# GpSimd makes 18 of the 198 low parts of the expert weights, VectorE the others

## Chip, core, metric

The kernel runs on one core of a Trainium2 chip. The metric is the device time of one execution in microseconds, the median of some runs. All arithmetic is float32 at the interface. TensorE multiplies in a reduced 32-bit format (fp32r), so the kernel splits each float32 operand into a high part, which is a copy in that format, and a low part, the rest, and adds two or three products.

## What is computed

Two residual layers. Each has a token mixer (gated short convolution beside latent attention). The first is followed by a dense SwiGLU, the second by eight SwiGLU experts of which each token uses two. The part that matters here is the last:

```
def moe_swiglu(x, w_router, w_gate, w_up, w_down):
    logits = (t @ w_router)
    top_vals, top_idx = lax.top_k(logits, 2)
    top_w = jax.nn.softmax(top_vals, axis=-1)
    gates = sum(one_hot(top_idx, 8) * top_w[..., None], axis=1)
    for e in range(8):
        out = out + gates[:, e:e+1] * ((silu(t @ w_gate[e]) * (t @ w_up[e])) @ w_down[e])
```

256 tokens, width 1024, expert width 1792. All eight experts' weights, 176 MB, are read once from memory.

## The kernel before

Each engine has its own program; nothing but semaphores orders them. Layer 0 and the mixer of layer 1 take the first 690 us or so. The expert part follows and is what the change touches.

**Steps and granules.** Experts are sorted on the chip by how many tokens chose them. The three with most tokens are computed for 128 tokens (large), the other five for 64 (small). Each expert is worked in two halves of its width of 1792; a half is a step k, 16 steps in a round. Steps 0, 1, 6, 7, 12, 13 are of large experts, 2 to 5, 8 to 11, 14 and 15 of small ones. One round serves all tokens unless an expert has too many; rounds 1 and 2 exist as code and are not run here. A granule is what one DMA loads: 128 rows of the gate matrix (n = 0 to 7) or of the up matrix (n = 8 to 15) with the 896 columns of this half, 448 KB, or 128 rows of the down matrix with 1024 columns (n = 16 to 22, 512 KB). Step k's list of granules is its 16 gate and up granules and then the seven down granules of step k - 1. The list of the round, GRANULES, has 368 entries.

**The path of a granule.** SP loads it into one of 12 raw slots (`expert_loads`). ACT copies it to the high part, in one of 8 weight slots (`expert_hi`, L943). DVE subtracts the high part from the raw one and writes the low part (`expert_lo`, L1491). PE multiplies with both. ACT and DVE take two neighbours at once where both have the same width: this is a split (SPLITS, 198 in the round), 128x1792 for gate and up, 128x2048 for down; where the widths differ each goes alone. The high part of a split waits for its loads and for PE's use of the granules that held the weight slots eight granules before. The low part waits for the high part (`e_hi_made`). PE waits for the low part (`e_lo_made`, counted in the order of the splits). SP's next load into a raw slot waits for the low part of the granule that lay there twelve before, and SP issues loads in their order, so that the loads behind a waiting one wait as well.

**DVE's order** is written out by its loop over the granules: at every second granule i it makes the low part of the split that is eight ahead, and between these stand the operations that drain the banks: `expert_hidden` (hid_buf, L1630, silu(gate) times up), `hidden_lo_half` (hT, L1636 and L1640, the low part of the transposed hidden values), `output_lo` (y_lo, L1613), `add_output` (h, L1620) and `choose` (sel, L1596). Each of these but the last has one input in PSUM; a low part L1491 reads raw and w_hi, both in SBUF. **GpSimd (POOL)** does small things for the norms, and in the expert part nothing until the final norm (L721).

## Time and profile before

| | |
|---|---|
| median of 3 runs | 1156.25 us (1156.22 to 1157.06) |
| the profiled execution | 1157.23 us, span 1155.4 us, granted clock 0.998 |
| busy over the span | PE 1125.5 us (97%), DVE 878.4 (76%), ACT 753.7 (65%), POOL 35.0 (3%) |
| costliest group of the expert part | L1491 on DVE, w_lo and w_lo_more, 198 operations, 383 us |
| chain that ended last | PE 75%, DVE 18%, DMA 3%, ACT 2% |

In the profile's rows a time is in microseconds from the start of the span, a duration in microseconds or, where marked ns, nanoseconds. "x2" is how many instructions a row holds. The records of DVE operations that follow each other overlap by some 0.07 us, so what one costs its engine is the distance from start to start. A busy PE is not PE at its peak, since the ends of its matmuls are modelled.

### The profile page before, as it was taken

To read this page: it belongs to the slowest core of one execution; us is meant where nothing else is said; L and a number is where in the kernel's file an instruction comes from. 1 tells how busy PE (TensorE), PEld (TensorE's weight loads), DVE (VectorE), ACT (ScalarE), POOL (GpSimd) and SP (SyncE) were. 2 spreads that over 40 slices of the span, in tenths; PEclk is the share of its full clock that TensorE was granted. 3 is DMA by queue.
4 is the path that set the end of the run, shared out by engine and by line. 5 is a ranking of instruction groups with operands and counts; after the bars stand their busy time and mean duration, and the time that the engine had idled before them with its cause. 6 is when DMAs were issued, how large, how long until landed. Compare 5 with 4: busy or idle time off the path is not lost.

```text
span 1155.4 us, 15714 instructions
## 1 busy us (share of the span) xinstructions
PE 1125.5 (97%) x5556; PEld 944.9 (82%) x5556; DVE 878.4 (76%) x986; ACT 753.7 (65%) x936; POOL 35.0 (3%) x64
## 2 busy tenths in 40 slices
PE   8999999999999999999999999999899999999997
PEld 7888788888888888888788888887778887888885
DVE  6568667665454555468667669999999899999997
ACT  6555566545444345555566556799987798988785
POOL 3001000000000001001001000000000000000000
PEclk9999999999999999999999999999999999999999
DMA  8845433668556344645433556999999999999993
GB/s 302 298 135 182 146 103 111 190 210 305 186 183 198 114 169 145 213 135 182 147 101 133 189 202 221 390 386 407 407 407 395 369 399 401 406 407 405 406 370 155
DMA packets 120555, 294.96 MB, mean 255 GB/s; under 512 B 9007, under 2 KB 33677, under 8 KB 119965
## 3 DMA queue, kind: packets, MB, share of 16 engines
q1 hardware_dynamic: 119376, 288.66, 69.3%
q0 software_dynamic: 960, 5.28, 1.2%
q8 instruction: 42, 0.69, 0.2%
q14 instruction: 37, 0.30, 0.1%
q10 hardware_dynamic: 140, 0.04, 0.0%
HBM read 292.90 MB, written 1.05 MB: 254 GB/s over the span
## 4 chain that ended last, share of the span: by engine, by line
PE 75%; DVE 18%; DMA 3%; ACT 2%; issue 2%; SPq 0%; ACTq 0%; DVEq 0%
PE bank L1716 21%; PE bank L1717 20%; PE bank L1718 20%; DVE w_lo L1491 10%; DVE w_lo_more L1491 3%; DMA raw<-in_moe_w_gate 2%; PE bank L2134 2%; PE bank L2135 2%; PE bank L1936 2%; PE bank L1760 2%; PE bank L1956 2%; PE bank L1944 1%; DVE hid_buf L1630 1%; PE bank L2117 1%; PE bank L1924 1%
## 5 line engine op out<-in xcount | busy, mean ns | idle before, releaser
L1161 DVE TENSOR_TENSOR w_lo<-raw,w_hi 128x1536 fp32r<-128x1536 f32 (+4 forms) x142 | 241.7, 1708 | 147.0 <-ACT w_hi L735 146.5
L735 ACT ACTIVATE w_hi<-raw 128x1536 fp32r<-128x1536 f32 (+5 forms) x142 | 202.4, 1432 | 156.6 <-PE bank L1718 154.1
L1491 DVE TENSOR_TENSOR w_lo<-raw,w_hi 128x1792 fp32r<-128x1792 f32 (+3 forms) x148 | 286.6, 1964 | 11.5 <-ACT w_hi L943 11.2
L943 ACT ACTIVATE w_hi<-raw 128x1792 fp32r<-128x1792 f32 (+3 forms) x148 | 244.5, 1668 | 46.8 <-PE bank L1718 30.0
L1716 PE MATMUL bank<-w_hi,aT_hi 128*128 128x512 f32 (+1 forms) x592 | 235.5, 398 | 0.2
L1718 PE MATMUL bank<-w_hi,aT_lo 128*128 128x512 f32 (+1 forms) x592 | 230.1, 389 | 0.0
L1717 PE MATMUL bank<-w_lo,aT_hi 128*128 128x512 f32 (+1 forms) x592 | 229.7, 388 | 0.0
L1718 PEld LDWEIGHTS bank<-w_hi,aT_lo 128*128 128x128 f32 x592 | 111.2, 188 | 22.6
L1716 PEld LDWEIGHTS bank<-w_hi,aT_hi 128*128 128x128 f32 x592 | 111.3, 188 | 22.3 <-DVE w_lo L1161 0.9
L1717 PEld LDWEIGHTS bank<-w_lo,aT_hi 128*128 128x128 f32 x592 | 111.4, 188 | 20.2
L1491 DVE TENSOR_TENSOR w_lo_more<-raw,w_hi_more 128x1792 fp32r<-128x1792 f32 (+3 forms) x50 | 96.7, 1941 | 6.1 <-ACT w_hi_more L943 6.1
L2134 PE MATMUL bank<-w_hi,xT 128*128 128x448 f32 x240 | 91.1, 380 | 6.1 <-DVE w_lo L1491 5.7
L943 ACT ACTIVATE w_hi_more<-raw 128x1792 fp32r<-128x1792 f32 (+3 forms) x50 | 82.0, 1649 | 11.5 <-PE bank L1718 7.3
L2135 PE MATMUL bank<-w_lo,xT 128*128 128x448 f32 x240 | 87.9, 366 | 0.0
L2134 PEld LDWEIGHTS bank<-w_hi,xT 128*128 128x128 f32 x240 | 45.1, 188 | 15.8 <-DVE w_lo L1491 11.2
L1717 PE MATMUL bank<-w_lo,hT_hi_buf 128*128 128x512 f32 x144 | 57.2, 397 | 0.0
L1716 PE MATMUL bank<-w_hi,hT_hi_buf 128*128 128x512 f32 x144 | 57.0, 396 | 0.0
L1718 PE MATMUL bank<-w_hi,hT_lo_buf 128*128 128x512 f32 x144 | 56.8, 394 | 0.0
L1716 PE MATMUL bank<-w_hi,bT_hi 128*128 128x512 f32 x128 | 51.8, 404 | 2.9 <-DVE w_lo L1161 2.9
L1716 PE MATMUL bank<-w_hi,xT 128*128 128x448 f32 x144 | 54.0, 375 | 0.5 <-DVE w_lo L1491 0.3
L1718 PE MATMUL bank<-w_hi,xT 128*128 128x448 f32 x144 | 52.9, 367 | 0.0
L1717 PE MATMUL bank<-w_lo,xT 128*128 128x448 f32 x144 | 52.8, 367 | 0.0
(327 smaller groups left out, 1803.8 us busy)
## 6 DMA issues: line engine op xcount, KB each, us to landing
raw<-in_moe_w_gate SPq DMA_DIRECT2D x128, 448.0 KB, 7.5
raw<-in_moe_w_up SPq DMA_DIRECT2D x128, 448.0 KB, 7.1
raw<-in_moe_w_down SPq DMA_DIRECT2D x112, 512.0 KB, 7.4
raw<-in_w_in SPq DMA_DIRECT2D x40, 768.0 KB, 4.6
raw<-in_dense_w_gate SPq DMA_DIRECT2D x22, 512.0 KB, 4.1
raw<-in_dense_w_up SPq DMA_DIRECT2D x22, 512.0 KB, 4.9
raw<-in_dense_w_down SPq DMA_DIRECT2D x11, 1024.0 KB, 5.1
raw<-in_w_in SPq DMA_DIRECT2D x20, 512.0 KB, 4.9
```

The lines of the kernel that those rows point to most:

```text
L735: act.activation(dst, src, ACT.Copy).then_inc(hi_made[j], 1)
L943: act.activation(split_of(hi_slot, m), raw_of(i, n), ACT.Copy).then_inc(e_hi_made, 1)
L1161: dve.tensor_tensor(dst, src, high, ALU.subtract).then_inc(lo_made[j], 1)
L1491: dve.tensor_tensor(split_of(lo_slot, m), raw_of(i, n), split_of(hi_slot, m).bitcast(F32), ALU.subtract).then_inc(e_lo_made, 1)
L1716: pe.matmul(dst, x_hi, b_hi, start=start, stop=False)
L1717: pe.matmul(dst, x_hi, b_lo, start=False, stop=False)
L1718: return pe.matmul(dst, x_lo, b_hi, start=False, stop=stop)
L1760: last = pe.transpose(bank[at_bank[n]][:, (c % 2) * S + t * P:(c % 2) * S + (t + 1) * P], src(t)[:, c * P:(c + 1) * P], ident[:, :])
L1936: last = pe.matmul(bank[B_S][:, t * P:(2 * t + 1) * P], qT[0:QK, t * P:(t + 1) * P], keys_of((n - 1) // 4)[0:QK, (n - 1) % 4, 0:(t + 1) * ...
L1956: last = pe.matmul(bank[B_O][:, t * VD:(t + 1) * VD], pT[:, m * P:(m + 1) * P], v[:, kt, (n - 3) * VD:(n - 2) * VD], start=start, stop=stop)
L2134: pe.matmul(dst, x, b_hi, start=start, stop=False)
L2135: return pe.matmul(dst, x, b_lo, start=False, stop=stop)
```

## The change

`low_by_pool(m)` names splits whose low part GpSimd makes: in round 0, in a step of a small expert other than the last step, a full pair that begins with n = 4 or 5 (of gate) or n = 12 or 13 (of up). These are two pairs in each of the steps 2, 3, 4, 5, 8, 9, 10, 11 and 14, 18 in all, each 128x1792. GpSimd makes them in their order after its last DMA and before the final norm's operations; each waits for its high part alone. DVE's `expert_lo` leaves them out. They count on a semaphore of their own, e_lo_pool. Everyone who waited for a low part (PE before its products, SP before a load, ACT and DVE before they overwrite raw slots at the end of the round) now waits on the counter of the engine that makes it, or at the end of the round on both.

```
+def low_by_pool(m):
+    r, k, n = GRANULES[SPLITS[m][0]]
+    return r == 0 and k < STEPS - 1 and is_small(k) and SPLITS[m][1] == 2 and n in (4, 5, 12, 13)
+POOL_LOWS = [m for m in range(len(SPLITS)) if low_by_pool(m)]
+def lows_through(m, by_pool):
+    return sum(low_by_pool(x) == by_pool for x in range(m + 1))
...
+        def wait_low(eng, m):
+            by_pool = low_by_pool(m)
+            eng.wait_ge(e_lo_pool if by_pool else e_lo_made, lows_through(m, by_pool))
+        def wait_lows_through(eng, m):
+            eng.wait_ge(e_lo_made, lows_through(m, False))
+            eng.wait_ge(e_lo_pool, lows_through(m, True))
...
-                                sp.wait_ge(e_lo_made, SPLIT_OF[RAW_BEFORE[i]] + 1)
+                                wait_low(sp, SPLIT_OF[RAW_BEFORE[i]])
...
+            for m in POOL_LOWS:
+                i, n = SPLITS[m]
+                pool.wait_ge(e_hi_made, m + 1)
+                pool.tensor_tensor(split_of(lo_slot, m), raw_of(i, n), split_of(hi_slot, m).bitcast(F32),
+                                   ALU.subtract).then_inc(e_lo_pool, 1)
             for t in range(NT):
                 pool.wait_ge(var_made, t + 1)
...
             def expert_lo(first):
                 for m in sorted({SPLIT_OF[first], SPLIT_OF[first + 1]}):
                     i, n = SPLITS[m]
+                    if low_by_pool(m):
+                        continue
...
-                pe.wait_ge(e_lo_made, SPLIT_OF[i] + 1)
+                wait_low(pe, SPLIT_OF[i])
```

The last pair of lines stands in all three places where PE waits for a low part. `h_slots_read` returns the split itself now, and its two callers use `wait_lows_through`.

DVE, the end of step 4 and the beginning of step 5, where both moved pairs of step 5 were made: before,

```order
526 L1630 TENSOR_TENSOR hid_buf<-sg_buf,bank 64x448 x2
527 L1491 TENSOR_TENSOR w_lo<-raw,w_hi 128x2x896
528 L1613 SCALAR_TENSOR_TENSOR y_lo<-bank,slot_gate,y_hi 128x512 x2
529 L1491 TENSOR_TENSOR w_lo<-raw,w_hi 128x2x896 x2
530 L1491 TENSOR_TENSOR w_lo_more<-raw,w_hi_more 128x2x896
531 L1596 TENSOR_SCALAR sel<-slot_no,slot_sorted 128x128 x4
532 L1636 TENSOR_TENSOR hT_hi_buf<-bank,hT_hi_buf 128x7x64
533 L1491 TENSOR_TENSOR w_lo<-raw,w_hi 128x2x896 x2
```

and after:

```order
524 L1662 TENSOR_TENSOR hid_buf<-sg_buf,bank 64x448 x2
525 L1645 SCALAR_TENSOR_TENSOR y_lo<-bank,slot_gate,y_hi 128x512 x2
526 L1523 TENSOR_TENSOR w_lo<-raw,w_hi 128x2x896 x2
527 L1523 TENSOR_TENSOR w_lo_more<-raw,w_hi_more 128x2x896
528 L1628 TENSOR_SCALAR sel<-slot_no,slot_sorted 128x128 x4
529 L1668 TENSOR_TENSOR hT_hi_buf<-bank,hT_hi_buf 128x7x64
530 L1523 TENSOR_TENSOR w_lo<-raw,w_hi 128x2x896
```

The low part between hid_buf and y_lo is gone, and one of the two behind hT.

DVE, the end of step 3 and the beginning of step 4, for the moved pairs of step 4: before,

```order
514 L1630 TENSOR_TENSOR hid_buf<-sg_buf,bank 64x448 x2
515 L1491 TENSOR_TENSOR w_lo<-raw,w_hi 128x2x896 x3
516 L1491 TENSOR_TENSOR w_lo_more<-raw,w_hi_more 128x2x896
517 L1491 TENSOR_TENSOR w_lo<-raw,w_hi 128x2x896
518 L1636 TENSOR_TENSOR hT_lo_buf<-bank,hT_lo_buf 128x7x64
519 L1491 TENSOR_TENSOR w_lo<-raw,w_hi 128x2x896
```

and after:

```order
513 L1662 TENSOR_TENSOR hid_buf<-sg_buf,bank 64x448 x2
514 L1523 TENSOR_TENSOR w_lo<-raw,w_hi 128x2x896 x2
515 L1523 TENSOR_TENSOR w_lo_more<-raw,w_hi_more 128x2x896
516 L1523 TENSOR_TENSOR w_lo<-raw,w_hi 128x2x896
517 L1668 TENSOR_TENSOR hT_lo_buf<-bank,hT_lo_buf 128x7x64
```

Here the second of the three low parts behind hid_buf is gone, with a low part on either side, and the one behind hT.

GpSimd, the end of its program, in the changed kernel:

```order
48 L743 DMA gain<-in_norm_final 128x1024 [waits gain_in,weighed]
49 L747 TENSOR_TENSOR w_lo<-raw,w_hi 128x2x896 [waits e_hi_made] x8
50 L747 TENSOR_TENSOR w_lo_more<-raw,w_hi_more 128x2x896 [waits e_hi_made] x2
51 L747 TENSOR_TENSOR w_lo<-raw,w_hi 128x2x896 [waits e_hi_made] x8
52 L751 TENSOR_TENSOR small<-small 128x1 [waits var_made] x2
```

Before, the last row stood right behind the DMA. The 18 subtracts are new.

## Rows read from the trace of the kernel before

**Rows 1.** The page's 40 slices, each 28.9 us: DMA share in tenths, rate.

```profile
DMA  8845433668556344645433556999999999999993
GB/s 302 298 135 182 146 103 111 190 210 305 186 183 198 114 169 145 213 135 182 147 101 133 189 202 221 390 386 407 407 407 395 369 399 401 406 407 405 406 370 155
```

**Rows 2.** Windows: stretch, length, busy PE, PEld, DVE, ACT, POOL, clock, DMA, GB/s.

```profile
757.00:870.00 113.00, 106.52 (x519) 88.27 (x518) 110.67 (x77) 102.52 (x106) 0.00 (x0) 1.00 1.02 404
870.00:930.00 60.00, 60.00 (x307) 53.60 (x306) 53.79 (x37) 48.23 (x52) 0.00 (x0) 1.00 1.00 378
930.00:1040.00 110.00, 105.61 (x516) 87.94 (x515) 108.95 (x78) 99.14 (x103) 0.00 (x0) 1.00 1.02 405
1040.00:1088.00 48.00, 48.00 (x236) 42.27 (x236) 44.40 (x30) 37.87 (x30) 0.00 (x0) 1.00 1.03 405
1088.00:1140.00 52.00, 50.88 (x236) 41.28 (x235) 51.75 (x36) 46.41 (x42) 0.00 (x0) 1.00 0.89 345
```

**Rows 3.** Windows of 10 us in steps 14 and 15, with the same columns.

```profile
1100.00:1110.00 10.00, 10.00 (x45) 8.21 (x44) 10.00 (x8) 7.79 (x7) 0.00 (x0) 1.00 1.02 381
1110.00:1120.00 10.00, 10.00 (x52) 8.39 (x52) 10.00 (x9) 9.21 (x10) 0.00 (x0) 1.00 0.96 361
1120.00:1130.00 10.00, 9.33 (x41) 7.08 (x40) 10.00 (x6) 9.84 (x9) 0.00 (x0) 1.00 0.97 381
```

**Rows 4.** Timeline of ACT: start, duration, operation, [idle before <- what ended it].

```profile
807.52 1.70 ACT L943 ACTIVATE w_hi_more<-raw 128x1792 fp32r<-128x1792 f32 x1 [0.57 <-DMA raw<-in_moe_w_up]
809.76 1.71 ACT L943 ACTIVATE w_hi<-raw 128x1792 fp32r<-128x1792 f32 x1 [0.54 <-DMA raw<-in_moe_w_up]
...
837.89 1.71 ACT L943 ACTIVATE w_hi<-raw 128x1792 fp32r<-128x1792 f32 x1
```

**Rows 5.** Timeline of DVE, the same columns, end of step 4, start of step 5.

```profile
830.35 1.13 DVE L1630 TENSOR_TENSOR hid_buf<-sg_buf,bank 64x448 f32<-64x448 f32 x2
831.41 2.01 DVE L1491 TENSOR_TENSOR w_lo<-raw,w_hi 128x1792 fp32r<-128x1792 f32 x1
833.34 1.39 DVE L1613 SCALAR_TENSOR_TENSOR y_lo<-bank,slot_gate,y_hi 128x512 fp32r<-128x512 f32 x2
834.67 3.94 DVE L1491 TENSOR_TENSOR w_lo<-raw,w_hi 128x1792 fp32r<-128x1792 f32 x2
...
840.47 0.86 DVE L1596 TENSOR_SCALAR sel<-slot_no,slot_sorted 128x128 fp32r<-128x128 f32 x4
841.25 0.61 DVE L1636 TENSOR_TENSOR hT_hi_buf<-bank,hT_hi_buf 128x448 fp32r<-128x448 f32 x1
841.79 2.00 DVE L1491 TENSOR_TENSOR w_lo<-raw,w_hi 128x1792 fp32r<-128x1792 f32 x1
```

**Rows 6.** DVE groups from 740 us: busy us, mean ns | idle before.

```profile
L1620 DVE TENSOR_TENSOR h<-h,bank 128x512 f32<-128x512 f32 x12 | 8.1, 674 | 0.0
```

**Rows 7.** Timelines of POOL and DVE at 98 us; the last row from 533 us.

```profile
98.21 3.68 POOL L702 COPY kT<-raw 32x3072 f32<-32x3072 f32 x1 [57.46 <-DVE bT_lo L1353]
101.84 2.02 POOL L702 COPY raw<-raw 32x1024 f32<-32x1024 f32 x1
...
98.06 1.22 DVE L1161 TENSOR_TENSOR w_lo<-raw,w_hi 128x1024 fp32r<-128x1024 f32 x1
99.20 1.40 DVE L1269 SCALAR_TENSOR_TENSOR gates<-bank,small,gates 128x512 f32<-128x512 f32 x2
100.71 2.26 DVE L1161 TENSOR_TENSOR w_lo<-raw,w_hi 128x1024 fp32r<-128x1024 f32 x1
103.53 1.42 DVE L1161 TENSOR_TENSOR w_lo<-raw,w_hi 128x1024 fp32r<-128x1024 f32 x1 [0.56 <-ACT w_hi L735]
...
533.86 2.26 DVE L1161 TENSOR_TENSOR w_lo<-raw,w_hi 128x1024 fp32r<-128x1024 f32 x1
```

**Rows 8.** The page's DMA issues: line, count, KB each, median us to landing.

```profile
raw<-in_moe_w_gate SPq DMA_DIRECT2D x128, 448.0 KB, 7.5
...
raw<-in_dense_w_gate SPq DMA_DIRECT2D x22, 512.0 KB, 4.1
```

More of the change, by code:

```diff
@@ L177, in h_slots_read @@
 def h_slots_read(r, slots):
-    return SPLIT_OF[max(i for i in range(PER_ROUND * r, PER_ROUND * (r + 1)) if (i + RAW_SLOTS // 2) % RAW_SLOTS in slots)] + 1
+    return SPLIT_OF[max(i for i in range(PER_ROUND * r, PER_ROUND * (r + 1)) if (i + RAW_SLOTS // 2) % RAW_SLOTS in slots)]
 RAW_BEFORE, W_BEFORE = slot_history(RAW_SLOTS), slot_history(W_SLOTS)
@@ L355, in build_trunk @@
         e_raw_in = [sem(f"e_raw_in{s}") for s in range(RAW_SLOTS)]
-        e_hi_made, e_lo_made, e_used, e_silu_made, e_hid_made, e_hid_tr, e_hT_hi_made, e_hT_lo_made = (sem(n) for n in (
-            "e_hi_made", "e_lo_made", "e_used", "e_silu_made", "e_hid_made", "e_hid_tr", "e_hT_hi_made", "e_hT_lo_made"))
+        e_hi_made, e_lo_made, e_lo_pool, e_used, e_silu_made, e_hid_made, e_hid_tr, e_hT_hi_made, e_hT_lo_made = (sem(n) for n in (
+            "e_hi_made", "e_lo_made", "e_lo_pool", "e_used", "e_silu_made", "e_hid_made", "e_hid_tr", "e_hT_hi_made", "e_hT_lo_made"))
         logits_made, lmax_made, lexp_made, rw_scaled, hT_act, hT_dve, ones_made, angle_made, sines_made = (sem(n) for n in (
@@ L1065, in residual_high @@
                 act.wait_ge(h_new, 4 + 4 * (PAIRS_E * r + PAIRS_E - 1))
-                act.wait_ge(e_lo_made, h_slots_read(r, H_SLOTS[0:2]))
+                wait_lows_through(act, h_slots_read(r, H_SLOTS[0:2]))
                 for t in range(NT):
@@ L1647, in residual_low @@
                     if t == 0:
-                        dve.wait_ge(e_lo_made, h_slots_read(r, H_SLOTS[2:4]))
+                        wait_lows_through(dve, h_slots_read(r, H_SLOTS[2:4]))
                     dve.tensor_tensor(h_lo[:, t, :], h[:, t, :], h_hi[:, t, :].bitcast(F32), ALU.subtract).then_inc(h_lo_made, 1)
@@ L2172, in down_granule @@
                     pe.wait_ge(e_hT_lo_made, 2 * (STEPS * r + k - 1) + c // 4 + 1)
-                pe.wait_ge(e_lo_made, SPLIT_OF[i] + 1)
+                wait_low(pe, SPLIT_OF[i])
                 part = slice(c * P, (c + 1) * P)
@@ L2189, in last_granules @@
                         i, cols_u = SEQ[r, k, GU_N + c], slice(u * NB, (u + 1) * NB)
-                        pe.wait_ge(e_lo_made, SPLIT_OF[i] + 1)
+                        wait_low(pe, SPLIT_OF[i])
                         last = small_product(bank[B_Y[u]][:, :], hT_lo_buf[:, c * P:(c + 1) * P], w_of(hi_slot, i)[:, cols_u], w_of(lo_slot, i)[:, cols_u],
```

## The prediction, made before the changed kernel was run

> **What bounds the kernel now.** I read the slices first [rows 1]: from slice 25 on, about 722 us, the expert part runs, and there the DMA row shows 9 tenths in nearly every slice, with around 400 GB/s. The windows [rows 2] show PE nearly full as well, so the share of busy time alone decides nothing. They cut that part by the size of the experts. In both long stretches of small experts (757 to 870 and 930 to 1040) the DMA runs at 404 and 405 GB/s, DVE is busy 110.67 of 113 us and 108.95 of 110, and PE leaves 6.5 and 4.4 us open. In the stretches of large experts (870 to 930, 1040 to 1088) PE is busy throughout and DVE leaves 6.2 and 3.6 us. The full slices repeat 405 to 407 GB/s and stop there [rows 1], which I take for the loads' limit. So in small experts two things end last together. ACT's timeline shows one: its high parts start every 2.25 us and wait each time for a landing [rows 4], so the loads pace it. DVE's own timeline shows the other: low part behind low part without a hole [rows 5]. DVE needs all but 3.6 us of the time that the DMA needs anyway: 2.33 + 1.05 + 0.25 us of idle in the three stretches of small experts [rows 2]. That is all the room into which new DVE time can go, and relief of DVE can bring only what the DMA still leaves.
>
> **What the change removes.** 18 low parts of 128x1792 leave DVE (9 half experts, two each). One costs 1.93 us from start to start (831.41 to 833.34, [rows 5]). That is 18 x 1.93 = 34.7 us less work in DVE's queue.
>
> **What it adds: a subtract on GpSimd.** The trace has no large GpSimd operation with two inputs. The nearest rows are the two copies of L702, and they show two things [rows 7]. The first is a shared resource. A DVE low part of 128x1024 takes 1.22 us; the one that starts at 100.71, while the copy is at work, takes 2.26 and ends at 102.97, that is 1.08 after the copy's end at 101.89. The second copy, listed from 101.84, then ends 0.89 us after that low part, at 103.86, and the next low part, begun at 103.53, takes 1.42 instead of 1.22, as if it had begun when this copy ended. The two operations of L1269 at 99.20, which have one input tensor in PSUM, take 1.40 for two beside the first copy, and are not held up. The pattern is there a second time from 531 us on, with 2.26 again for the held low part. So I read: a GpSimd operation that reads SBUF and a DVE operation with two SBUF inputs exclude each other for their whole length, in both directions, and DVE operations with one operand in PSUM run on. The low parts are of the excluded kind, and they are what the change puts beside each other. The second thing is the rate: the first copy was itself held until the low part of 98.06 ended at 99.28, and then moved 3072 elements in 2.61 us, 0.85 ns each; the second 1024 in 0.89.
>
> The price of one subtract of 1792 elements has these bounds. Below: both inputs through one port at the copy's working rate, 2 x 0.85 x 1792 = 3.05 us. Above: the copy's whole record, 3.68 us for 3072, doubled, 4.29 us. I take 3.8 us, above the middle of 3.67, since a copy does no arithmetic and its rate is a floor. On this the trace is thin. The Trainium skill, page "GPSIMD Engine Reference", section "Performance versus the Vector engine", gives 4497 ns for a tensor_tensor of 2048 elements; scaled to 1792 that is an estimate of 3.9 us, and the sum below would come out 2.4 us later. The page "SBUF — State Buffer", section "Who interferes with whom", states the exclusion that I read from the copies; were it untrue for a subtract, the sum would turn into the first rival below.
>
> **The sum in the critical place.** With exclusion, each subtract holds DVE's next low part for 3.8 us where the low part on DVE took 1.93: gross 18 x (3.8 - 1.93) = 33.7 us.
>
> Part of it is covered by DVE operations that don't need the port, if the subtract runs beside them. From the order of the changed program and the start-to-start times [rows 5]: at the first moved pair of steps 3, 5, 9 and 11 stand hid_buf before (1.06 us) and y_lo after (1.33): 4 x 2.39 = 9.6 us. At their second pair stands hT (0.54), in steps 5 and 9 also sel (0.78): 3.7 us. At the second pair of step 4 stands hT, 0.5 us, and of steps 10 and 14 two additions to h each (674 ns by record [rows 6], 0.60 from start to start, since the other records too are 0.07 longer than that): 2.4 us. The first pairs of steps 2, 4, 8, 10 and 14 have low parts on both sides and no cover. In all 16.2 us. The cover needs the subtract to start where its place is. It starts when its high part is there, and where DVE runs behind that is earlier, in front of a low part: in step 5 the high part of the second pair ends at 839.60 and its low part stands at 841.79 [rows 4, 5], 2.2 us, more than one low part. A DVE that the subtracts delay falls further behind. I count three quarters of the cover, 12.2 us.
>
> DVE's idle time takes up 3.6 us. Left: 33.7 - 12.2 - 3.6 = **17.9 us**. It is not given back in the large experts: there PE is full [rows 2], and starts later by what DVE lost.
>
> The rest costs nothing or nearly so. GpSimd is idle in all of that time [rows 2], and nothing but the two closing operations of the norm stands behind the subtracts in its queue. SP waits for the low part that frees a raw slot, in order, and behind it stand the next loads: a low part that is late by up to a few us is covered by the loads under way. They land after a median of 7.5 us against 4.1 for 512 KB in the dense part, where the DMA is not full [rows 1, 8], so some 3.4 us of queue are there. The split of one counter into two (e_lo_made, e_lo_pool) adds one wait in two places at the end of the round, on low parts made long before: nothing on this scale. If the queue's cover of 3.4 us were gone, each us beyond it would idle the DMA directly; that is the fourth case.
>
> The profiled execution took 1157.23 us, span 1155.4 and 1.8 outside it, and lies 1.0 above the median of 1156.25. So 1157.2 + 17.9 = 1175.1 for such an execution and **1174 us** for the median. The bounds: 3.05 us a subtract and full cover give 18 x 1.12 - 16.2 - 3.6 = 0.4, 1157; 4.29 us and half the cover give 42.5 - 8.1 - 3.6 = 30.8, 1187.
>
> **Rivals.** First, **no exclusion** between this subtract and the low parts (the copies have another reason, such as their 32 partitions or their own source). Then DVE is relieved of 34.7 us, more than 3 us in every small step, and the DMA's limit decides. It yields what separates the windows from 407 GB/s: 113 x 3/407 = 0.8, 110 x 2/407 = 0.5, and in 1100 to 1130, with 381, 361 and 381 while DVE is full [rows 3], 30 - 1123/407 x 10 = 2.4 us. 3.7 us less, 1152.5. It decides the sign as soon as DVE's records in the changed kernel are as long as before. For it speaks only that the excluded operation in the trace is a copy; against it both occurrences of the pattern. Chance 0.12.
>
> Second, **a cheap subtract with full cover**: exclusion holds, but the price is near 3.0 and the subtracts fall into the gaps: 1156 to 1157, no difference. Chance 0.07.
>
> Third, my forecast, exclusion with a price of 3.05 to 4.29: chance 0.75.
>
> Fourth, **the subtract is starved**: DVE keeps the port while low parts queue. Runs of three are common, 5.8 us (834.67 to 840.47, [rows 5]), then 3.8 of its own, so the part is made 9.6 us after its high part where DVE took up to 2.2 + 1.9. That is 5.5 later, 2.1 beyond the 3.4 us that the loads cover; in half of the 18 places 19 us on top of the forecast, 1193. Against it: the low part of 100.71 got the port as soon as the first copy let go although the second copy was queued [rows 7], so whoever waits seems to be next. Chance 0.06.
>
> **How the numbers follow.** Forecast 1174, the likeliest case. Its own bounds, 1157 to 1187, hold 0.75. The range must also take in the second rival and part of the first and fourth: 1154 to 1192, which holds 0.8 or a little more. A measurement of this kernel can tell 0.2%, 2.3 us, from no change. Slower by more than that: 0.75 less 0.03 at the low bound, plus 0.06, 0.78. Within: 0.07 and 0.03, 0.10. Faster: 0.12.
>
> **What would show it.** In the changed profile: 18 subtracts on POOL of about 3.8 us, longer where they begin inside a DVE low part; DVE low parts of 128x1792 beside them of 3 to 5.7 us instead of 2.01, those elsewhere unchanged; DVE's busy time hardly lower although it has 18 operations less; DMA below 400 GB/s from 757 to 1040; PE waiting for lows, those of POOL among them. The part before 750 us unchanged. DVE records all at 2.01, with DVE 30 us less busy, would prove the exclusion wrong; subtracts that start 4 us or more after their high part, behind runs of low parts, would prove the fourth case; subtracts of 5 us or more beside idle DVE would prove the price wrong.

## The result and the profile after

The changed kernel takes 1183.6 us, the median of 4 runs (1181.0 to 1184.85), against 1156.3 for the kernel before (4 runs, 1156.22 to 1157.06). The ratio is 1.0228, with an interval of 1.0215 to 1.0240. So the change costs 27.3 us. The prediction said 1174 (1154 to 1192), slower. The profiled execution took 1183.14 us, its span 1181.3, which is 25.9 us more than the span before.

The page of the changed kernel: busy time of the engines, the rates in the 40 slices (each 29.5 us), four of the costliest groups, one DMA row.

```profile
PE 1134.3 (96%) x5556; PEld 950.5 (80%) x5556; DVE 884.1 (75%) x968; ACT 754.6 (64%) x936; POOL 118.3 (10%) x82
...
GB/s 306 289 134 171 167 99 111 193 236 264 203 186 178 150 139 162 199 130 187 125 90 167 225 139 366 350 337 395 407 395 366 341 341 361 372 409 406 382 374 137
...
L1523 DVE TENSOR_TENSOR w_lo<-raw,w_hi 128x1792 fp32r<-128x1792 f32 (+3 forms) x132 | 283.7, 2177 | 22.7 <-ACT w_hi L973 22.3
...
L2166 PE MATMUL bank<-w_hi,xT 128*128 128x448 f32 x240 | 94.9, 395 | 22.8 <-POOL w_lo L747 13.2
...
L747 POOL TENSOR_TENSOR w_lo<-raw,w_hi 128x1792 fp32r<-128x1792 f32 x16 | 75.3, 4704 | 265.5 <-ACT w_hi L973 265.5
...
raw<-in_moe_w_gate SPq DMA_DIRECT2D x128, 448.0 KB, 6.4
```

DVE has 18 operations fewer and is not less busy: 884.1 us against 878.4 on the page of before. 34.7 us of low parts went away, so 884.1 - 878.4 + 34.7 = 40.4 us came back as time in which DVE was held inside its own records. The rates of the slices 26 and 27 are 350 and 337 GB/s where they were 390 and 386, those of 32 to 35 are 341 to 372 where they were 369 to 406 [rows 1]. Landings take 6.4 us instead of 7.5 [rows 8]: the loads queue less.

Windows of the changed kernel: the two long stretches of small experts and the first of large ones, and 6 us of the first. Columns as in [rows 2]; the third number from the end is the granted share of TensorE's clock.

```profile
743.00:863.00 120.00, 107.44 (x499) 88.42 (x498) 108.83 (x64) 100.71 (x104) 35.94 (x8) 0.96 0.98 373
863.00:920.00 57.00, 57.00 (x293) 50.80 (x292) 52.91 (x39) 44.03 (x46) 0.00 (x0) 1.00 1.00 380
920.00:1044.00 124.00, 111.30 (x523) 92.23 (x522) 111.48 (x69) 101.00 (x106) 38.92 (x8) 0.97 0.95 357
766.00:772.00 6.00, 4.98 (x14) 4.46 (x15) 5.77 (x5) 2.14 (x2) 0.00 (x0) 0.50 0.90 314
```

I cut both programs at the same high parts, from the first of each group of small steps to the third of the large step behind it. The steps 2 to 5 take 120.3 us instead of 112.0, 8 to 11 take 124.1 instead of 112.65, and the steps 14 and 15 with the end 85.3 instead of 82.1: 8.3 + 11.5 + 3.2 = 23.0 of the 25.9 us. The large experts add 2.4, and 0.6 us lies ahead of step 2, where nothing was changed. In these three stretches DVE's idle time was 3.7, 3.0 and 8.6 us and is now 11.2, 12.5 and 11.1, that is 19.5 us more. The prediction let it shrink by 3.6. TensorE is idle more, too, and its clock is at half for a while: the windows of before show a full clock in this part [rows 2], here 17.1 us run at 1.2 GHz.

The subtracts on GpSimd, in order of time: an unheld one, the three longest and the last of the first group. Columns as in [rows 4].

```profile
753.13 4.07 POOL L747 TENSOR_TENSOR w_lo<-raw,w_hi 128x1792 fp32r<-128x1792 f32 x1 [62.10 <-ACT w_hi L973]
...
811.90 5.70 POOL L747 TENSOR_TENSOR w_lo<-raw,w_hi 128x1792 fp32r<-128x1792 f32 x1 [13.75 <-ACT w_hi L973]
822.22 5.03 POOL L747 TENSOR_TENSOR w_lo<-raw,w_hi 128x1792 fp32r<-128x1792 f32 x1 [4.62 <-ACT w_hi L973]
...
849.91 4.04 POOL L747 TENSOR_TENSOR w_lo<-raw,w_hi 128x1792 fp32r<-128x1792 f32 x1 [6.22 <-ACT w_hi L973]
...
989.05 8.71 POOL L747 TENSOR_TENSOR w_lo<-raw,w_hi 128x1792 fp32r<-128x1792 f32 x1 [13.89 <-ACT w_hi L973]
```

Ten of the 18 take 4.03 to 4.09 us: that is the price of an undisturbed one. The others are held by DVE. DVE's timeline in the same execution:

```profile
755.27 3.82 DVE L1523 TENSOR_TENSOR w_lo_more<-raw,w_hi_more 128x1792 fp32r<-128x1792 f32 x1 [2.96 <-ACT w_hi_more L973]
759.01 2.01 DVE L1523 TENSOR_TENSOR w_lo<-raw,w_hi 128x1792 fp32r<-128x1792 f32 x1
760.95 0.68 DVE L1672 TENSOR_TENSOR hT_lo_buf<-bank,hT_hi_buf 128x512 fp32r<-128x512 f32 x1
761.54 5.42 DVE L1523 TENSOR_TENSOR w_lo<-raw,w_hi 128x1792 fp32r<-128x1792 f32 x1
...
811.70 2.01 DVE L1523 TENSOR_TENSOR w_lo<-raw,w_hi 128x1792 fp32r<-128x1792 f32 x1
...
849.38 4.66 DVE L1628 TENSOR_SCALAR sel<-slot_no,slot_sorted 128x128 fp32r<-128x128 f32 x4
```

The low part of 755.27 begins while the subtract of 753.13 is at work. That one ends at 757.20, and the low part ends 1.89 us later, at 759.09. The one of 761.54 waits in the same way for the subtract of 761.04, which ends at 765.08. In the other direction the subtract of 811.90 begins inside a low part that ends at 813.71 and ends 3.89 us later. That is the exclusion of the prediction, to two tenths of a microsecond. The last row is one that I had not expected: the four small sel operations, 0.86 us before [rows 5], take 4.66 beside the subtract of 849.91, since one of them takes 4.07.

What a late low part does is seen in TensorE's timeline, with one row of ACT's behind it:

```profile
763.14 0.56 PE L2174 MATMUL bank<-fold,shift 128*128 128x448 f32 x2
767.02 0.74 PE L2166 MATMUL bank<-w_hi,xT 128*128 128x448 f32 x1 [3.32 <-DVE w_lo L1523]
767.56 0.57 PE L2167 MATMUL bank<-w_lo,xT 128*128 128x448 f32 x1
767.93 0.57 PE L2166 MATMUL bank<-w_hi,xT 128*128 128x448 f32 x1
...
770.49 1.91 ACT L973 ACTIVATE w_hi<-raw 128x2048 fp32r<-128x2048 f32 x1 [3.86 <-PE bank L2167]
```

TensorE stands for 3.32 us until the held low part of 761.54 is there. Its products then start every 0.37 us, at 1.2 GHz, where they started every 0.20 before the hole. Meanwhile no weight slot comes free, so ACT stands for 3.86 us and makes no high parts, and DVE, once it has worked off what was ready, waits for high parts at 772, 775, 778 and 780 us, for 0.3 to 0.9 us each. Before, no hole of TensorE from 740 to 1150 us was 1.2 us long. Now there are eight, of 3.32, 1.97, 2.02, 3.33, 1.60, 1.25, 3.13 and 1.26 us, 17.9 us together.

The waits of the changed kernel from 740 to 1145 us: engine and line, what it waited for, us in total, times, the longest.

```profile
DVE w_lo L1523 <- ACT w_hi L973: 20.5, 20, 3.0
ACT w_hi L973 <- PE bank L2167: 19.5, 19, 5.8
PEld bank L2166 <- POOL w_lo L747: 17.0, 11, 3.5
PEld bank L2166 <- DVE w_lo L1523: 14.4, 14, 3.7
```

In the kernel before the first two were 9.0 and 6.1 us. The ring of weight slots closes: DVE waits for ACT, ACT for TensorE, TensorE for DVE and GpSimd.

### The profile page after: what moved, and what is told of

It reads as the page before. It is cut to its first block, busy times and chain, and to the rows that moved or that the text cites. A ratio compares the mean times of both kernels' runs of the same rounds, so it can differ in the third digit from the quotient of the medians.

```text
span 1181.3 us, 15714 instructions
## 1 busy us (share of the span) xinstructions
PE 1134.3 (96%) x5556; PEld 950.5 (80%) x5556; DVE 884.1 (75%) x968; ACT 754.6 (64%) x936; POOL 118.3 (10%) x82
## 4 chain that ended last, share of the span: by engine, by line
PE 74%; DVE 16%; ACT 3%; DMA 2%; issue 2%; POOL 1%; SPq 0%; ACTq 0%; DVEq 0%
PE bank L1748 20%; PE bank L1749 20%; PE bank L1750 20%; DVE w_lo L1523 8%; DVE w_lo_more L1523 3%; PE bank L2166 3%; PE bank L2167 2%; PE bank L1968 2%; PE bank L1792 2%; PE bank L1988 1%; ACT w_hi L973 1%; POOL w_lo L747 1%; DMA raw<-in_w_in 1%; PE bank L1976 1%; DVE sel L1628 1%
## 5 line engine op out<-in xcount | busy, mean ns | idle before, releaser
L1523 DVE TENSOR_TENSOR w_lo<-raw,w_hi 128x1792 fp32r<-128x1792 f32 (+3 forms) x132 | 283.7, 2177 | 22.7 <-ACT w_hi L973 22.3
L2166 PE MATMUL bank<-w_hi,xT 128*128 128x448 f32 x240 | 94.9, 395 | 22.8 <-POOL w_lo L747 13.2
L747 POOL TENSOR_TENSOR w_lo<-raw,w_hi 128x1792 fp32r<-128x1792 f32 x16 | 75.3, 4704 | 265.5 <-ACT w_hi L973 265.5
L2167 PE MATMUL bank<-w_lo,xT 128*128 128x448 f32 x240 | 90.5, 377 | 0.0
L1748 PE MATMUL bank<-w_hi,xT 128*128 128x448 f32 x144 | 53.8, 373 | 0.2 <-DVE xT L1698 0.2
L1750 PE MATMUL bank<-w_hi,xT 128*128 128x448 f32 x144 | 52.7, 366 | 0.0
```

Source lines behind the costliest of these rows:

```text
L747: pool.tensor_tensor(split_of(lo_slot, m), raw_of(i, n), split_of(hi_slot, m).bitcast(F32), ALU.subtract).then_inc(e_lo_pool, 1)
L1523: dve.tensor_tensor(split_of(lo_slot, m), raw_of(i, n), split_of(hi_slot, m).bitcast(F32), ALU.subtract).then_inc(e_lo_made, 1)
L1748: pe.matmul(dst, x_hi, b_hi, start=start, stop=False)
L1750: return pe.matmul(dst, x_lo, b_hi, start=False, stop=stop)
L2166: pe.matmul(dst, x, b_hi, start=start, stop=False)
L2167: return pe.matmul(dst, x, b_lo, start=False, stop=stop)
```

## The experiments

The changed kernel does three things at once: it takes 18 low parts off DVE, it holds the port that DVE needs, and it makes 18 parts later. The first runs take these apart. All ratios are against the kernel before, run on the same chip (medians 1156.5 to 1157.0), with 95% intervals.

| kernel | what GpSimd does | time, us | ratio |
|---|---|---|---|
| relief | nothing | 1155.61 | 0.9995 [0.9985, 1.0004] |
| late | two memsets, 3.3 us | 1157.46 | 1.0009 [0.9999, 1.0019] |
| late3 | three memsets, 4.9 us | 1163.71 | 1.0058 [1.0041, 1.0075] |
| port | a constant subtract, 3.2 us, not waited for | 1165.92 | 1.0074 [1.0052, 1.0096] |
| port2 | a constant subtract, 4.0 us, not waited for | 1183.01 | 1.0226 [1.0208, 1.0243] |
| port_pe | as port2, TensorE waits for it | 1186.53 | 1.0258 [1.0238, 1.0278] |
| order | the subtract, behind DVE's previous low part | 1184.64 | 1.0242 [1.0225, 1.0259] |
| halves | the subtract in two halves | 1192.93 | 1.0317 [1.0300, 1.0334] |
| keep | the subtract; TensorE gets filler products | 1184.52 | 1.0230 [1.0209, 1.0251] |
| covered | 4 subtracts, where most cover was counted | 1157.07 | 1.0002 [0.9992, 1.0012] |
| bare | 5 subtracts, where none was counted | 1166.67 | 1.0083 [1.0066, 1.0100] |
| drop3 | 15 subtracts, without three places | 1169.86 | 1.0114 [1.0097, 1.0131] |

### Relief alone

The 18 low parts are made by nobody. Whoever waited for them waits for the high part. In wait_low and in GpSimd's program:

```
-            by_pool = low_by_pool(m)
-            eng.wait_ge(e_lo_pool if by_pool else e_lo_made, lows_through(m, by_pool))
+            if low_by_pool(m):
+                eng.wait_ge(e_hi_made, m + 1)
+            else:
+                eng.wait_ge(e_lo_made, lows_through(m, False))
...
-            for m in POOL_LOWS:
```

> The 18 low parts are made by nobody: VectorE leaves them out, GpSimd does nothing for them, and whoever waited for one waits for its high part instead (the products then read an older low part). It measures what relief of VectorE alone is worth. Theory 'port' (the loss comes from GpSimd's subtracts and VectorE's low parts excluding each other) and theory 'late' (the loss comes from a low part that GpSimd delivers later than VectorE would, with or without exclusion) both expect 1150 to 1156 us, since the loads at some 407 GB/s leave 3.7 us. If it is under 1148 the loads are not the limit that I took them for.

1155.61 us, no gain that can be told. The windows of this kernel in the two long stretches of small experts:

```profile
757.00:870.00 113.00, 106.45 (x516) 89.23 (x516) 98.55 (x70) 101.71 (x106) 0.00 (x0) 0.98 1.02 400
930.00:1040.00 110.00, 106.34 (x523) 88.83 (x522) 97.65 (x71) 100.09 (x103) 0.00 (x0) 1.00 1.03 406
```

DVE has 12.1 and 11.3 us less to do than in [rows 2], and the DMA still moves 400 and 406 GB/s. That is what loads that end last look like, and a change that relieves DVE has nothing to win. The 3.7 us that the first rival hoped for are not there either.

### Lateness alone

GpSimd fills the low part with zeros, twice or three times over, instead of subtracting. It reads nothing, and whoever needs the part waits as in the changed kernel.

```
                 pool.wait_ge(e_hi_made, m + 1)
-                pool.tensor_tensor(split_of(lo_slot, m), raw_of(i, n), split_of(hi_slot, m).bitcast(F32),
-                                   ALU.subtract).then_inc(e_lo_pool, 1)
+                link(pool.memset(split_of(lo_slot, m).bitcast(F32), 0.0))
+                pool.memset(split_of(lo_slot, m).bitcast(F32), 0.0).then_inc(e_lo_pool, 1)
```

> The changed kernel with the subtract replaced by two memsets of the same tile, one after the other (some 4 us together by the rate of the 128x384 memset, 408 ns; the values are zeros and the rest of the high part is lost). GpSimd's part comes as late as in the changed kernel, but reads nothing from SBUF. Theory 'port' expects VectorE's records unchanged at 2.01 us and 1152 to 1160 us. Theory 'late' expects 1173 to 1184.

> As 'late' with three memsets one after the other, about 4.9 us, since two took 3.26 us only and GpSimd's subtract in the changed kernel 4.7 on the mean, held time included. No SBUF read on GpSimd, the part as late as there. If lateness costs by itself: 1163 to 1175 us. If it costs only together with low parts that VectorE cannot make meanwhile: 1156 to 1160.

GpSimd's timeline in late, and the group of DVE's low parts in late:

```profile
752.54 1.59 POOL L747 MEMSET w_lo<- 128x1792 f32 x1 [62.07 <-ACT w_hi L973]
754.19 1.60 POOL L748 MEMSET w_lo<- 128x1792 f32 x1
...
L1523 DVE TENSOR_TENSOR w_lo<-raw,w_hi 128x1792 fp32r<-128x1792 f32 (+3 forms) x132 | 255.6, 1962 | 32.1 <-ACT w_hi L973 31.4
```

DVE's 132 low parts take 255.6 us, to the tenth what they take in relief: a GpSimd operation that only writes holds nobody. A part that is ready 3.3 us after its high part costs 1.0 us in all, within what can be told from nothing; one that takes 4.9 us, more than the 4.63 us that the 18 subtracts take on average, costs 7.1. In late3 TensorE has a hole of 3.20 us at 836 us. So lateness of this size explains about a quarter of the 27.3 us, and it begins to cost somewhere between 3.3 and 4.9 us. Four of the subtracts, of 4.94 to 8.71 us, are later than any part here.

### Holding the port alone

GpSimd subtracts a constant tile from itself into a scratch tile at each of the 18 places. The low parts are left out as in relief, and nobody waits for GpSimd. The scratch tile lies where the gain of the last norm goes, so the load of that gain is issued behind the 18. In port the operation has 1792 elements, in port2 2304:

```
+                link(pool.tensor_tensor(scratch[:, :].bitcast(mybir.dt.bfloat16).rearrange("p (a b) -> p a b", b=P), ident[:, :].unsqueeze(1).to_broadcast([P, 18, P]),
+                                   ident[:, :].unsqueeze(1).to_broadcast([P, 18, P]), ALU.subtract))
```

> As the kernel in which nobody makes the 18 low parts, but at the same 18 places GpSimd subtracts 1792 elements of a constant tile from themselves into a scratch tile (bfloat16, for want of space), for which nobody waits. The port is used as in the changed kernel, no part is late. Theory 'port' expects most of the loss: 1172 to 1184 us, with VectorE's low parts beside the subtracts lengthened to 3 to 6 us. Theory 'late' expects the time of the kernel without the 18 parts, 1150 to 1157.

> As the run 'port', but GpSimd subtracts 2304 elements where it were 1792, since the constant subtract took 3.17 us and that of the changed kernel 4.05. Now the port is held as long as in the changed kernel and still nobody waits for GpSimd. If the loss follows the time on the port alone, 18 x 0.9 us more on it bring it near the changed kernel: 1176 to 1184 us. If a good part of the loss needs somebody to wait for GpSimd's result, 1167 to 1173.

Port, at 1165.92, fell between the two ranges that I had given for it. An unheld one takes 3.17 us there, too short to stand for the real one, so port2 was made longer. Its second place, GpSimd's row and DVE's:

```profile
760.90 4.21 POOL L748 TENSOR_TENSOR scratch<-ident 128x2304 bf16<-128x2304 f32 x1 [3.50 <-ACT w_hi L975]
...
761.74 5.25 DVE L1525 TENSOR_TENSOR w_lo<-raw,w_hi 128x1792 fp32r<-128x1792 f32 x1
```

This is the picture of the changed kernel again, without anyone who waits for GpSimd. Port2 loses 26.4 us, nearly the whole loss. From port to port2 the price of one operation rises by 4.03 - 3.17 = 0.86 us, 18 x 0.86 = 15.5 us, and the loss by 17.0, from 9.4 to 26.4: in this range each microsecond that a subtract gets longer is paid in full. (The rows are those of one execution, which for port2 was the slowest of four, 1187.73 us.) Port_pe gives TensorE's wait back, on top of port2:

```
-                wait_low(pe, SPLIT_OF[i])
+                wait_low_real(pe, SPLIT_OF[i])
```

> As 'port2', and TensorE waits for the constant subtract of its pair as it waits for the low part in the changed kernel; SP's loads do not (they wait for the high part). If TensorE's wait makes the rest of the loss, it is as slow as the changed kernel: 1180 to 1187 us. If it is SP's wait, and so the loads, that makes it, the time stays that of 'port2'.

It adds 3.5 us, and with 30.0 us loses 2.7 more than the changed kernel; why more, no run shows. A port held for 4 us and lateness do not add up: 26.4 and up to 7 alone, 27.3 in the changed kernel.

### Is it the wrong order of two parts?

At 761 us the subtract of a pair that is needed later goes ahead of a low part on DVE that is needed first. One theory was that this inversion makes the holes. In order, GpSimd also waits until DVE has made the low part before its own:

```
                 pool.wait_ge(e_hi_made, m + 1)
+                pool.wait_ge(e_lo_made, lows_through(m - 1, False))
```

> The changed kernel in which each subtract also waits until VectorE has finished the low part in front of it, so that it never goes ahead of a part that TensorE needs sooner. In the trace of the changed kernel three subtracts did that (at 761, 939 and 1116 us), and two of the three largest jumps of the delay, 4.8 and 4.1 us, stand there. Theory 'inversion' (these two places cost some 9 us by themselves) expects 1173 to 1177 us. Theory 'port' without it, where only the time on the port counts, expects 1181 to 1186, as before the edit.

1184.64 us, no better. The second place in this kernel, GpSimd's row and DVE's:

```profile
763.10 4.73 POOL L748 TENSOR_TENSOR w_lo<-raw,w_hi 128x1792 fp32r<-128x1792 f32 x1 [6.49 <-ACT w_hi_more L974]
...
760.95 2.01 DVE L1524 TENSOR_TENSOR w_lo<-raw,w_hi 128x1792 fp32r<-128x1792 f32 x1
762.88 6.03 DVE L1524 TENSOR_TENSOR w_lo_more<-raw,w_hi_more 128x896 fp32r<-128x896 f32 x2
```

DVE's part of 760.95 is now on time (2.01 us), and the subtract starts 2 us later. It holds the next low parts instead, 6.03 us for two that take 2.2, and TensorE stands for 3.00 us at 764.88, for GpSimd's part this time. The theory falls: it doesn't matter which of the two comes first, since the port is held for 4 us either way.

### Is the hold too long in one piece?

In halves each subtract is two of 896 elements, of about 2.1 us each when unheld.

```
-                pool.tensor_tensor(split_of(lo_slot, m), raw_of(i, n), split_of(hi_slot, m).bitcast(F32),
-                                   ALU.subtract).then_inc(e_lo_pool, 1)
+                for x in range(n):
+                    last = pool.tensor_tensor(w_of(lo_slot, i + x), raw_of(i + x)[:, 0, :], w_of(hi_slot, i + x).bitcast(F32), ALU.subtract)
+                last.then_inc(e_lo_pool, 1)
```

> The changed kernel with each subtract cut into two of 896 elements, one granule each, so that the port comes free in the middle and VectorE's waiting low part can take it. If the loss follows the sum of GpSimd's time on the port: 1182 to 1188 us (a little more for the second start). If it follows the length of one hold, because only a hold longer than what the ring of eight weight slots can bridge makes TensorE stand: 1160 to 1172.

1192.93 us, 36.0 above the kernel before, 8.7 worse than the changed kernel and outside both ranges. The worst place, GpSimd's two halves and DVE beside them:

```profile
838.67 11.51 POOL L748 TENSOR_TENSOR w_lo<-raw,w_hi 128x896 fp32r<-128x896 f32 x2 [10.17 <-ACT w_hi L974]
...
841.05 1.40 DVE L1646 SCALAR_TENSOR_TENSOR y_lo<-bank,slot_gate,y_hi 128x512 fp32r<-128x512 f32 x2
842.37 3.94 DVE L1524 TENSOR_TENSOR w_lo<-raw,w_hi 128x1792 fp32r<-128x1792 f32 x2
846.24 2.01 DVE L1524 TENSOR_TENSOR w_lo_more<-raw,w_hi_more 128x1792 fp32r<-128x1792 f32 x1
848.17 2.68 DVE L1629 TENSOR_SCALAR sel<-slot_no,slot_sorted 128x128 fp32r<-128x128 f32 x4
```

Three low parts of DVE, from 842.37 to 848.25, take their normal 1.93 us each: they weren't held, so the second half didn't have the port. The part took 11.5 us, and TensorE stood for 8.22 us. A cut lets DVE in between, and a part that is needed comes later still.

### What does the half clock cost?

In keep, 24 small products run ahead of TensorE's wait at four places where it had a hole or stood near one. They go into unused columns of a bank whose sums are under way, and part of what is computed is lost by that; the work and its waits are all there.

```
+                if SPLITS[SPLIT_OF[i]][0] == i and i < PER_ROUND and SPLIT_OF[i] in FILLED:
+                    for _ in range(24):
+                        pe.matmul(bank[(B_GATE, B_UP)[n // KC][0]][:, HN:NB], ident_r[:, :], ident_r[:, 0:NB - HN], start=True, stop=True, skip_group_check=True)
```

> The changed kernel, with 24 small products (64 columns, into unused columns of the bank) on TensorE ahead of four waits, those in front of which TensorE stood 2.0 to 3.3 us in the trace of the changed kernel (at 763.7, 841.7, 941.6 and 994.7 us). Behind each of the four the granted clock fell to half for 3.4 or 6.8 us, 17 us in all. Theory 'clock' (part of the loss is TensorE at 1.2 GHz behind a hole) expects no or fewer such stretches and 1174 to 1180 us, since 17 us at half speed are up to 8.5 us of work. Theory 'no clock' (TensorE is not what ends last there, the low parts are) expects 1182 to 1188.

1184.52 us in all, but the first place did what was wanted. The window of keep that answers to the 0.50 above:

```profile
764.00:772.00 8.00, 7.27 (x47) 6.78 (x47) 8.00 (x6) 5.57 (x6) 0.60 (x1) 1.00 0.91 318
```

The clock stays at 2.4 GHz there, and until step 4 this kernel is 4.4 us behind the kernel before, where the changed one is 7.0 behind. Later it gets other holes (3.88 us at 812.63, 3.02 at 998.75) and 20.5 us of half clock instead of 17.1, 6.8 of them from 945.5 us on, right behind one of the fillers. So at one place, in one execution of each, the clock is worth 2.6 us. The time of the whole lies in the range of the theory that the clock costs nothing, but since there was no less of the half clock, the run decides nothing. The most it can be is what 17.1 us at half the rate lose, 8.5 us. That share stays open between near nothing and 8.5. In the traces the half clock comes with the loss, none of it before 1145 us in covered and late, 6.8 us in port, 10.2 in bare, 27.3 in halves; but relief has 3.4 us of it, from 848 us on, and loses nothing.

### Where is it lost?

Three kernels move only some of the 18 pairs:

```
covered: and SPLITS[m][1] == 2 and n == 4
bare:    and SPLITS[m][1] == 2 and n == 5
drop3:   and SPLITS[m][1] == 2 and n in (4, 5, 12, 13) and m not in (27, 102, 123)
```

Covered has the first pairs of the steps 3, 5, 9 and 11, where the prediction counted hid_buf and y_lo as cover. Bare has the first pairs of 2, 4, 8, 10 and 14, without cover. Drop3 is the changed kernel without the second pairs of the steps 2 and 8 and the first of step 10.

> Of the 18 subtracts only the four at the first pair of steps 3, 5, 9 and 11, which stand between hid_buf and y_lo on VectorE; the other 14 low parts go back to VectorE. By the prediction's terms with the measured price of 4.05: 4 x (4.05 - 1.93 - 2.39) = -1.1 us, so 1155 to 1157. If a GpSimd subtract costs something wherever it stands: 1159 to 1164.

> Only the five subtracts at the first pair of steps 2, 4, 8, 10 and 14, which have low parts on both sides and no cover. By the prediction's terms 5 x (4.05 - 1.93) = 10.6 us less at most some idle: 1163 to 1167. By the jumps in the trace of the changed kernel (about 1 us at step 4 and 3.7 at step 10, none at 2, 8 and 14): 1160 to 1162.

> The changed kernel without three of the 18: the second pairs of steps 2 and 8 and the first of step 10, where the trace of the changed kernel shows its three largest jumps of the delay (4.8, 4.1 and 3.7 us) and, two of them, a hole of 3.3 us on TensorE. If the loss sits in these places: 12.6 us less, 1169 to 1173. If every subtract bears its share: 27.3 x 15/18 = 22.8 us, 1178 to 1180.

Covered loses nothing (1157.07 us), bare 9.7 us with five subtracts, and drop3 12.9 where the changed kernel loses 27.3: half of the loss hangs on three of 18 places. One of the three, the first pair of step 10, is also among bare's five. From first high part to first high part, step 10 takes 4.6 us longer in bare than before, and the steps of the other four 1.2 to 1.6 each. The best place, in covered, GpSimd's row and DVE's:

```profile
776.36 4.12 POOL L747 TENSOR_TENSOR w_lo<-raw,w_hi 128x1792 fp32r<-128x1792 f32 x1 [86.21 <-ACT w_hi L973]
...
776.46 1.14 DVE L1662 TENSOR_TENSOR hid_buf<-sg_buf,bank 64x448 f32<-64x448 f32 x2
778.06 1.41 DVE L1645 SCALAR_TENSOR_TENSOR y_lo<-bank,slot_gate,y_hi 128x512 fp32r<-128x512 f32 x2 [0.47 <-ACT y_hi L1090]
780.23 2.13 DVE L1523 TENSOR_TENSOR w_lo<-raw,w_hi 128x1792 fp32r<-128x1792 f32 x1 [0.76 <-ACT w_hi L973]
```

The subtract runs beside operations with an operand in PSUM and beside two short pauses, and the next low part is held for only 0.1 us. In bare, at the first pair of step 8, it is the opposite; GpSimd's row and DVE's:

```profile
975.77 8.19 POOL L747 TENSOR_TENSOR w_lo<-raw,w_hi 128x1792 fp32r<-128x1792 f32 x1 [48.70 <-ACT w_hi L973]
...
976.17 2.01 DVE L1523 TENSOR_TENSOR w_lo<-raw,w_hi 128x1792 fp32r<-128x1792 f32 x1
978.10 2.01 DVE L1523 TENSOR_TENSOR w_lo_more<-raw,w_hi_more 128x1792 fp32r<-128x1792 f32 x1
980.04 0.67 DVE L1652 TENSOR_TENSOR h<-h,bank 128x512 f32<-128x512 f32 x1
980.63 5.21 DVE L1523 TENSOR_TENSOR w_lo<-raw,w_hi 128x1792 fp32r<-128x1792 f32 x1
```

The subtract is recorded from 975.77, yet two low parts run unheld. It gets the port when h leaves it free at 980.04, and the next low part is held to 985.84. The part takes 8.19 us, and TensorE stands for 3.12 us at 980.89. The changed kernel has the same at 989.05. Nor are these two all: in seven of the ten kernels in which GpSimd subtracts there are 13 operations during which whole low parts of DVE, begun later, ran unheld. Port, where nobody waits for GpSimd, has two. One merged row of GpSimd holds the second of them, 10.36 us, and the operation behind it; DVE's row is the last of three low parts that ran unheld meanwhile:

```profile
978.93 15.28 POOL L748 TENSOR_TENSOR scratch<-ident 128x1792 bf16<-128x1792 f32 x2 [13.96 <-ACT w_hi L975]
...
984.24 2.01 DVE L1525 TENSOR_TENSOR w_lo<-raw,w_hi 128x1792 fp32r<-128x1792 f32 x1
```

In all 13 the GpSimd record begins beside an operation of DVE with an operand in PSUM, or at most 0.3 us behind the start of a low part, and low parts follow without a pause. In order, at 812.21, a subtract that begins 0.2 us behind the start of a low part gets the port right after that one, so this is no rule. What such a delay costs can be seen in bare: 4.6 us at step 10, where the places without it cost 1.2 to 1.6.

No version that moves subtracts to GpSimd was faster than the kernel before, and relief says that none of this kind can be by much.

## Why the prediction was right, and where it was too small

**The mechanism and the sign** were right. The rows of the two copies [rows 7] showed the exclusion, and it holds for a subtract in both directions. The range held the time. The size was short: 17.9 us were forecast, 27.3 came. By its own terms:

**The price of a subtract**, 3.8 us between 3.05 and 4.29, is 4.03 to 4.09 where nothing holds it. At 4.05 the gross becomes 18 x 2.12 = 38.2 us instead of 33.7: 4.5 us of the 9.4 that were missing. The estimate from the Trainium skill, "GPSIMD Engine Reference", section "Performance versus the Vector engine", was 3.9 us, and nearer. The lesson is in the bounds: I had put the value above the middle since a copy does no arithmetic, and it should have been nearer still to the upper bound.

**Cover and idle time**, together 15.8 us, were worth 38.2 - 27.3 = 10.9. The two kernels that only hold the port leave nearly the same remainder: port 18 x (3.17 - 1.93) - 9.4 = 12.9, port2 18 x (4.03 - 1.93) - 26.4 = 11.4. So the remainder is about 11 to 13 us whatever the price, and this is the rest of the error, 4.9 us. It is the right sum for partly wrong reasons, as the records show. DVE was held for 40.4 us, where my terms give 18 x 3.8 - 12.2 = 56.2. Against that its idle time in the small steps grew by 19.5 us, where I had it shrink by 3.6. 40.4 + 19.5 - 34.7 = 25.2 us, against 25.9 in the span. By the records some 32 of the 40 us are held low parts, and 7.6 are sel. The step that failed is the one that treats DVE's time as a store to be filled. A hold of 3 to 4 us in one piece makes one part late, TensorE stands, no slot comes free, and DVE then idles for want of high parts. While it idles, the next subtract costs it nothing; that this is why it was held less than forecast is my reading, which no run tests by itself.

**The cover, place by place.** The first pairs of the steps 3, 5, 9 and 11 were put at 4 x (3.8 - 1.93) - 9.6 = -2.1 us with the whole cover, so nothing, and covered shows nothing. The pairs without cover were put at 1.87 us each, 10.6 us for five at the measured price, and bare shows 9.7. The account of sel was wrong: it isn't cover, it is held itself, 4.66 us instead of 0.86. No run moves the nine second pairs alone. If the parts added up, 27.3 - 9.7 - 0.1 = 17.5 us would be theirs, where the terms with the measured price and the whole cover give 9 x 2.12 - 6.6 = 12.5; about half of that stands at two places: without them the steps 2 and 8 take 4.5 and 3.8 us less in drop3 than in the changed kernel. And bare's 9.7 agree with 10.6 partly by luck: by its traces four of the five places cost 1.2 to 1.6 us each and not 2.12, and the fifth, where the subtract is starved, 4.6.

**"GpSimd's waits cost nothing or nearly so"** was right for the loads and wrong for TensorE. The prediction spoke of raw slots and of 3.4 us in the DMA's queue. The holes are at the products, and late3 shows that parts 4.9 us behind their high part cost 7 us with nobody held. I didn't ask how far ahead of TensorE a low part is made.

**TensorE's clock** doesn't appear in the prediction at all. It is worth up to 8.5 us here, 2.6 of them seen at one place. I read it as a part of DVE's idle time and not as an extra on top, since the account above closes without it and a slower TensorE frees slots later; no run shows that by itself.

**The rivals.** No exclusion is ruled out by the first row of DVE's timeline, and its 3.7 us of gain by relief. The starved subtract, at 0.06, happened at one place of 18 (989.05), where it was to happen at half of them. Against it I had argued that whoever waits is next, from a copy that was queued [rows 7]. The 13 cases above show that this doesn't always hold; in port two of the 18 took 8.64 and 10.36 us instead of 3.17. It is a part of the loss, some 3 us at step 10, and not the bulk.

**What would show it** came as listed, with one exception: DVE low parts of 3 to 5.7 us (3.08 to 5.43), DMA below 400 GB/s, waits of TensorE for both makers of low parts. The exception is the length of the subtracts beside busy low parts, up to 8.71 us.

## What to carry to other kernels

Before work is moved to relieve an engine, leave it out in a trial kernel and see what the relief can bring at most: here one run would have said that there was nothing to win. GpSimd is no free place for a subtract of two SBUF tensors beside a DVE that makes such subtracts, because each excludes the other for its whole length and GpSimd's is twice as long; it cost nothing only beside DVE operations with an operand in PSUM, or beside pauses. And where a ring of slots closes through several engines, count how late a single item gets and not only the sums of busy time: at the same 18 places operations cost 1 us when a part came after 3.3 us and held nobody, and 26 us when they held the port for 4.

## What the runs showed of the hardware

- A DVE TENSOR_SCALAR of 128x128 f32 with one tensor input in SBUF (its scalar is one value per partition, also in SBUF) is held by a GpSimd subtract like an operation with two (one of the four sel takes 4.07 us, and the four 4.66 instead of 0.86); additions and products with an operand in PSUM are not.
- A subtract of 128x1792 on GpSimd takes 4.05 us with two f32 tensors. One of two broadcast constant tiles into bf16 takes 3.17 us at that size and 4.03 at 2304 elements. A memset of 1792 elements takes 1.60 us and doesn't hold DVE.
- The subtract of 989.05 in the changed kernel was recorded 0.9 us before DVE's low part of 989.96 began, with an operation on a PSUM operand in between, and still the low part ran unheld in 2.02 us. The Trainium skill, "SBUF — State Buffer", section "Who interferes with whom", says that issue order decides who blocks and, of the two-port modes of VectorE, that whoever issues first gets the shared ports for the whole instruction. Thirteen such cases (one in the changed kernel and in bare, two each in keep, port, port2 and port_pe, three in halves) don't fit if the record's start is the issue; what happens in the time between is open, and no run here resolved it.
- TensorE went to 1.2 GHz four times in the changed kernel before its end, for 17.1 us together: at 765.8 us for 6.8 us, and at 844.3, 946.7 and 997.9 for 3.4 us each. Before that it had stood for 3.32, 2.02, 3.33 and 3.13 us, from 763.70, 841.73, 941.57 and 994.69. Holes of this size don't decide it alone: after 1.97 us at 815.68 the clock stayed at 2.4 GHz, and after 2.33 us at 831.31 in covered; after 1.97 us at 809.48 in bare and 1.78 at 845.31 in relief it fell, and in keep it fell at 945.5 behind 24 filler products and a wait of 0.71 us.
